# Two joined transformer blocks on one core: experts that add into the residual, and a layer norm inside the next feed-forward

## The reference, cut to what matters

```python
x = layer_norm(ALPHA * x + (1 + gt1) * mix, ln1_g, ln1_b)     # ALPHA = 2 ** 0.25
h = x * (1 + sc2) + sh2
ffn = moe_ffn(h, router_w, router_b, w1, b1, w2, b2)          # 32 experts, 1024 -> 2048 -> 1024
x = layer_norm(ALPHA * x + (1 + gt2) * ffn, ln2_g, ln2_b)
# second model, two layers
h = rmsnorm(x, ffn1_norm[i])
x = x + 0.5 * (silu(h @ wg) * (h @ wu)) @ wd                  # 1024 -> 2816 -> 1024
x = x + mixing(rmsnorm(x, mix_norm[i]), positions, ...)       # fox, dilated (rope), hgrn2
x = x + 0.5 * swiglu(rmsnorm(x, ffn2_norm[i]))
# layer_norm: (x - mean) / sqrt(var + 1e-5) * g + b ; rmsnorm: x / sqrt(mean(x*x) + 1e-6) * g
# softmax over layers of hgrn_lower_bounds, and cos/sin of positions: computed once ("tables")
```

## Time and profile before

| | |
|---|---|
| median of 3 runs | 2408.95 us (2402.76 to 2416.14) |
| profiled execution | span 2405.4 us, first to last instruction; no time of its own is shown beside it |
| TensorE (PE) busy | 2217.6 us, 92% |
| VectorE (DVE) busy | 1085.6 us, 45% |
| ScalarE (ACT) busy | 709.9 us, 30% |
| DMA | 626.63 MB, mean 261 GB/s; about 425 GB/s in the expert stage |

### The profile page before, as it was taken

The page is one execution under the profiler, slowest core; times in us unless marked ns, Lnnn a source line. Parts: engine busy times, 40 slices in busy tenths (PEclk is TensorE's granted clock), DMA queues, the critical chain, the costliest instruction groups (busy, mean ns, idle before and its releaser), DMA issues. The chain is left out here.

```text
span 2405.4 us, 37789 instructions
## 1 busy us (share of the span) xinstructions
PE 2217.6 (92%) x15750; PEld 1605.7 (67%) x15750; DVE 1085.6 (45%) x1633; ACT 709.9 (30%) x899; POOL 18.7 (1%) x17
## 2 busy tenths in 40 slices
PE   6987879999999999999996999999999999999998
PEld 4746743443333333333335999988999999988997
DVE  4548342121111111111115656677656656677664
ACT  3343231111111111111114444445334434445332
POOL 0002000000000000000000000000000000000000
PEclk8968989999999999999998999999999999999999
DMA  9630269999999999999985455424555555424551
GB/s 391 241 158 27 69 281 424 424 425 426 425 425 425 425 425 425 425 426 425 418 334 169 158 192 175 134 95 140 193 182 168 193 187 181 139 90 140 194 188 56
DMA packets 233056, 626.63 MB, mean 261 GB/s; under 512 B 13144, under 2 KB 149880, under 8 KB 197112
## 3 DMA queue, kind: packets, MB, share of 16 engines
q1 hardware_dynamic: 229736, 622.06, 67.2%
q10 hardware_dynamic: 3216, 3.06, 0.4%
HBM read 624.03 MB, written 1.05 MB: 260 GB/s over the span
## 5 line engine op out<-in xcount | busy, mean ns | idle before, releaser
L1916 DVE TENSOR_TENSOR w_low<-ring,w_high 128x2048 fp32r<-128x2048 f32 x168 | 383.8, 2290 | 274.9 <-ACT w_high L1911 274.9
L1911 ACT ACTIVATE w_high<-ring 128x2048 fp32r<-128x2048 f32 x168 | 319.8, 1909 | 269.7 <-PE bank L2125 136.6
L1672 PE MATMUL bank<-ring,ut 128*64 128x512 f32 x1024 | 250.6, 642 | 47.2 <-DMA ring<-in_exp_w_dram 47.2
L1643 PE MATMUL bank<-ring_odd,xt 128*64 128x512 f32 x1024 | 225.0, 597 | 0.0
L1643 PE MATMUL bank<-ring,xt 128*64 128x512 f32 x1024 | 223.3, 594 | 0.3 <-ACT xt L1726 0.3
L1672 PEld LDWEIGHTS bank<-ring,ut 128*64 128x64 f32 x1024 | 73.5, 146 | 208.6 <-issue 126.7
L2140 PE MATMUL bank<-h_high,w_high 128*128 128x256 f32 x1408 | 186.8, 281 | 16.0 <-ACT h_high L2013 16.0
L2140 PEld LDWEIGHTS bank<-h_high,w_high 128*128 128x128 f32 x1408 | 175.4, 189 | 16.8 <-ACT h_high L2013 16.6
L2140 PE MATMUL bank<-h_high,w_low 128*128 128x256 f32 x1408 | 185.9, 280 | 0.0
L2140 PE MATMUL bank<-h_low,w_high 128*128 128x256 f32 x1408 | 185.8, 280 | 0.0
L1730 ACT ACTIVATE sg<-glu 128x512 f32<-128x512 f32 x32 | 20.2, 630 | 537.4 <-DVE glu L1793 537.4
(11 more groups left out here) (532 smaller groups left out, 2871.3 us busy)
## 6 DMA issues: line engine op xcount, KB each, us to landing
ring<-in_exp_w_dram SPq DMA_DIRECT2D x256, 1024.0 KB, 21.8
ring_odd<-in_exp_w_dram SPq DMA_DIRECT2D x128, 1024.0 KB, 20.7
ring<-in_ffn_w_gate_dram SPq DMA_DIRECT2D x44, 1024.0 KB, 5.2
ring<-in_ffn_w_up_dram SPq DMA_DIRECT2D x44, 1024.0 KB, 5.2
ring<-in_ffn_w_down_dram SPq DMA_DIRECT2D x44, 1024.0 KB, 4.8
ring<-in_w_in_dram SPq DMA_DIRECT2D x36, 1024.0 KB, 5.3
ring<-in_ada_w_dram SPq DMA_DIRECT2D x24, 1024.0 KB, 12.3
ring<-in_w_out_dram SPq DMA_DIRECT2D x8, 1024.0 KB, 5.2
```

What stands on the lines that cost most here:

```text
L1643: ins = nc.tensor.matmul(bank[b][at:at + SLOTS, :], xt[:, c, SLOTS * side:SLOTS * side + SLOTS], (ring, ring_odd)[side][:, c, 512 * q:512 ...
L1672: ins = nc.tensor.matmul(bank[2 + dh][64 * dh:64 * dh + 64, :], ut[:, r % 4, 64 * (r // 4):64 * (r // 4) + 64], w[:, x, 512 * dh:512 * dh ...
L1911: nc.scalar.activation(w_bufs[0][u % BUFS], ring2[:, u % RING2, :], ACT.Copy).then_inc(high2, 1)
L1916: nc.vector.tensor_tensor(w_bufs[1][u % BUFS], ring2[:, u % RING2, :], w_bufs[0][u % BUFS].bitcast(F32), ALU.subtract).then_inc(low2, 1)
```

## The change

1. *Experts add into the scaled residual.* ALPHA is folded into the first norm's gain and bias (`x_gain`), the cleared accumulator is gone (its memset too), and each piece of `back` is now added by two operations of 128x256, piece times `mod` plus `xT`.
2. *Last second weights in first-weight slots.* The second weights of experts 30 and 31 go to `ring` slots 0 to 7 and wait for expert 30's first weights to be used, instead of slots 8 to 11 behind the second weights before them.
3. *Second layer norm inside the first feed-forward.* Stage c9 is gone. `opening` runs in the feed-forward's stage: VectorE halves the sum over chunks twice, so the mean is 2 products instead of 8; pairs of squares are added, so the variance is 4 instead of 8. Gain and bias of the norm times the RMS gain (`open_gain`) give `h_high` straight from the scaled `xT`; gain and bias are applied to `xT` by VectorE for even chunks and by ScalarE for odd ones.
4. *Tables over four units.* The tables are cut into four parts behind units 29 to 32; ScalarE's two functions come behind unit 32. `rope_tables` is cut in two for it.

```diff
@@ -1491,12 +1489,13 @@
+                act.wait_ge(sem("x_gain_ready"), 1)
-                    nc.scalar.activation(xT[:, c, :], xT[:, c, :], ACT.Identity, bias=par("ln1_b", c), scale=par("ln1_g", c))
+                    nc.scalar.activation(xT[:, c, :], xT[:, c, :], ACT.Identity, bias=x_gain[:, 1, c:c + 1], scale=x_gain[:, 0, c:c + 1])
...
@@ -1504,6 +1503,8 @@
+                nc.vector.tensor_scalar(x_gain[:, 0, :], par("ln1_g", 0, DC), ALPHA, None, ALU.mult)
+                st.tell(nc.vector.tensor_scalar(x_gain[:, 1, :], par("ln1_b", 0, DC), ALPHA, None, ALU.mult), "x_gain_ready")
@@ -1599,17 +1600,27 @@
-                    load_down(E - 2)
-                    load_down(E - 1)
+                    for k in range(8):
+                        sp.wait_ge(used, p * (8 * E) + (8 * E + (U_EXP - 16 + k + 1)))
+                        src = A["exp_w2"][0, E - 2 + k // 4, T * (k % 4):T * (k % 4) + T, :]
+                        sp.dma_start(slot3(k, 2), src.rearrange("(x p) n -> p x n", p=P)).then_inc(loaded[k], 16)
-                        load_up(E, 0)
+                        for k in range(8):
+                            sp.wait_ge(used_down, p * (4 * E) + (4 * (E - 2) + k + 1))
+                            sp.dma_start(ring[:, k, :], A["exp_w1"][0, 0, P * k:P * k + P, :]).then_inc(loaded[k], 16)
-                    def landed(k, e):
-                        pe.wait_ge(loaded[k], p * (16 * E) + (e * 16 + 16 * (loads_into(k, U_EXP) + 1)))
+                    def down_slot(e, k):
+                        if isinstance(e, int) and e >= E - 2:
+                            slot = 4 * (e - (E - 2)) + k
+                            pe.wait_ge(loaded[slot], p * (8 * E + 16) + (8 * E + 16 * (loads_into(slot, U_EXP) + 1)))
+                            return slot
+                        pe.wait_ge(loaded[8 + k], p * (16 * (E - 2)) + (e * 16 + 16 * (loads_into(8 + k, U_EXP) + 1)))
+                        return 8 + k
@@ -1664,8 +1675,7 @@
-                            landed(8 + k, e)
-                            w = slot3(8 + k, 2)
+                            w = slot3(down_slot(e, k), 2)
@@ -1804,8 +1814,11 @@
-                            av = flat(acc[:, 2 * n:2 * n + 2, :])
-                            nc.vector.tensor_tensor(av, bank[6 + n % 2][:, :], av, ALU.add).then_inc(sem("acc_added"), 1)
+                            for j in range(2):
+                                m = 2 * n + j
+                                ins = nc.vector.scalar_tensor_tensor(xT[:, m, :], bank[6 + n % 2][:, T * j:T * j + T], mod[:, 40 + m:41 + m], xT[:, m, :],
+                                                                     ALU.mult, ALU.add)
+                            ins.then_inc(sem("acc_added"), 1)
@@ -1914,52 +1927,6 @@
-        with ExitStack() as c9, Stage(nc, pool) as S:
...
-            ln_pe, ln_act, ln_dve = layer_norm(S, xT, root[:, :], sq, (0, 1))
...
-                ln_pe(pe)
...
-                    nc.scalar.activation(xT[:, 4 * j:4 * j + 4, :], xT[:, 4 * j:4 * j + 4, :], ACT.Copy, scale=ALPHA).then_inc(sem("x_scaled"), 1)
-                split_high(act, 0)
-                ln_act(act)
...
-                split_high(act, 1)
...
-                    st.tell(nc.vector.scalar_tensor_tensor(xT[:, m, :], acc[:, m, :], mod[:, 40 + m:41 + m], xT[:, m, :],
...
-                split_low(dve, 0)
-                ln_dve(dve, st)
-                split_low(dve, 1)
...
@@ -2073,7 +2041,77 @@
-        def ffn(S, f, L, base_unit, norm_name, first, flip, update, after, tables=None):
+        def opening(S, f):
+            sem = S.sem
+            mean, var = bank[6][:, 0:T], bank[7][:, 0:T]
+            halves = qp[:, :, :]
+            def tensor(pe):
+                pe.wait_ge(sem("halves_added"), 2)
+                for c in range(2):
+                    ins = nc.tensor.matmul(mean, ones, halves[:, c, :], start=(c == 0), stop=(c == 1))
+                ins.then_inc(sem("mean_ready"), 1)
+                for c in range(4):
+                    pe.wait_ge(sem("pairs_added"), c // 2 + 1)
+                    ins = nc.tensor.matmul(var, ones, squares[:, 4 * (c // 2) + c % 2, :], start=(c == 0), stop=(c == 3))
+                ins.then_inc(sem("var_ready"), 1)
+            def scalar(act):
+                for j in range(4):
+                    act.wait_ge(sem("centered"), j + 1)
+                    nc.scalar.activation(squares[:, 2 * j:2 * j + 2, :], xT[:, 2 * j:2 * j + 2, :], ACT.Square).then_inc(sem("squares"), 1)
+                split_high(act, 0)
+                act.wait_ge(sem("var_ready"), 1)
+                nc.scalar.activation(root[:, :], var, ACT.Sqrt, bias=1e-5, scale=1.0 / D).then_inc(sem("root_ready"), 1)
+                for c in range(DC):
+                    act.wait_ge(sem("scaled"), c // 2 + 1)
+                    nc.scalar.activation(h_parts[0][:, c, :], xT[:, c, :], ACT.Identity, bias=open_gain[:, 1, c:c + 1],
+                                         scale=open_gain[:, 0, c:c + 1]).then_inc(sem(f + "h_high"), 1)
+                    if c % 2:
+                        nc.scalar.activation(xT[:, c, :], xT[:, c, :], ACT.Identity, bias=par("ln2_b", c), scale=par("ln2_g", c)
+                                             ).then_inc(sem("x_odd"), 1)
+                split_high(act, 1)
+                for j in range(4):
+                    act.wait_ge(sem("x_even"), j + 1)
+                    act.wait_ge(sem("x_odd"), j + 1)
+                    nc.scalar.activation(squares[:, 2 * j:2 * j + 2, :], xT[:, 2 * j:2 * j + 2, :], ACT.Square).then_inc(sem(f + "squares"), 1)
+            def vector(dve):
+                st = Steps(dve, sem, "dve_step")
+                st.tell(nc.vector.memset(fox_bias[:, :], 0.0), "bias_cleared")
+                st.step(nc.vector.tensor_tensor(halves, xT[:, 0:4, :], xT[:, 4:8, :], ALU.add), "halves_added")
+                st.step(nc.vector.tensor_tensor(halves[:, 0:2, :], halves[:, 0:2, :], halves[:, 2:4, :], ALU.add), "halves_added")
+                for k, name in enumerate(("ln2_g", "ln2_b")):
+                    nc.vector.tensor_tensor(open_gain[:, k, :], par(name, 0, DC), par("ffn1_norm_2", 0, DC), ALU.mult)
+                dve.wait_ge(sem("mean_ready"), 1)
+                for j in range(4):
+                    xj = xT[:, 2 * j:2 * j + 2, :]
+                    st.tell(nc.vector.scalar_tensor_tensor(xj, mean.unsqueeze(1).to_broadcast([P, 2, T]), -1.0 / D, xj, ALU.mult, ALU.add), "centered")
+                for k in range(2):
+                    dve.wait_ge(sem("squares"), 2 * k + 2)
+                    st.tell(nc.vector.tensor_tensor(squares[:, 4 * k:4 * k + 2, :], squares[:, 4 * k:4 * k + 2, :], squares[:, 4 * k + 2:4 * k + 4, :],
+                                                    ALU.add), "pairs_added")
+                dve.wait_ge(sem("root_ready"), 1)
+                st.step(nc.vector.reciprocal(root[:, :], root[:, :]))
+                for j in range(4):
+                    xj = xT[:, 2 * j:2 * j + 2, :]
+                    st.tell(nc.vector.tensor_tensor(xj, xj, root[:, :].unsqueeze(1).to_broadcast([P, 2, T]), ALU.mult), "scaled")
+                    if j == 1:
+                        split_low(dve, 0)
+                for c in range(DC):
+                    dve.wait_ge(sem(f + "h_high"), c + 1)
+                    if c % 2:
+                        dve.wait_ge(sem("x_odd"), c // 2 + 1)
+                    else:
+                        st.step(nc.vector.tensor_scalar(xT[:, c, :], xT[:, c, :], par("ln2_g", c), par("ln2_b", c), ALU.mult, ALU.add), "x_even")
+                    nc.vector.scalar_tensor_tensor(h_parts[1][:, c, :], xT[:, c, :], par("ffn1_norm_2", c), h_parts[0][:, c, :].bitcast(F32),
+                                                   ALU.mult, ALU.subtract).then_inc(sem(f + "h_low"), 1)
+                split_low(dve, 1)
+            return tensor, scalar, vector
+        def ffn(S, f, L, base_unit, norm_name, first, flip, update, after, tables=None, opens=None):
@@ -2177,16 +2217,19 @@
-                parts_high(act)
+                if opens:
+                    opens[1](act)
+                else:
+                    parts_high(act)
-                if tables:
-                    tables[0](act)
+                    if tables and n == FFN_UNITS - 1:
+                        tables[0](act)
@@ -2228,18 +2271,21 @@
-                parts_low(dve, update)
+                if opens:
+                    opens[2](dve)
+                else:
+                    parts_low(dve, update)
-                if tables:
-                    tables[1](dve)
+                    if tables:
+                        tables[1](dve, n - (LOOP_AT + REPS * LOOP2))
@@ -2764,30 +2810,35 @@
-            def vector(dve):
-                st = Steps(dve, sem, "table_step")
-                dve.wait_ge(small, 16 * 9)
+            def vector(dve, part):
+                st = Steps(dve, sem, f"table_step{part}")
```

(27 more changed lines are left out.)

75 lines of the change are left out of this document (28 added, 47 removed).

## The result

Twenty runs of each kernel: before 2405.58 us (2401.23 to 2418.53), after 2392.44 us (2385.30 to 2401.69), ratio 0.9940, 95% interval 0.9926 to 0.9954. The median is 13.1 us lower, and the interval of the ratio stands for 11 to 18 us; 13.8 had been forecast from the profile, and 2395 as the time.

A forecast was written before the change was run, and what follows sets the result against it. Weights' DMAs pace the expert stage, TensorE what follows, where other work shows as holes. Opening with tail 10.3 plus tables 3.5 gave 13.8 us off, span 2391.6, time 2395; own range 2392 to 2399, with rivals A, B, D and scatter 2384 to 2407.

The forecast's parts named there:

- Expert tail: End of the expert stage: longer adds against new slots' -0.8 us; 0.45 us later at worst, range -0.4 to +1.3.
- The adds' term: Adds behind the expert loop: +0.5 us at the last but one back, +0.45 at the last add.
- Adds in the loop: Expert loop: some 0.5 us a back reaches TensorE but goes into the DMA wait of 3.0 us for two experts.
- Rival C: Expert loop: adds uncovered, 1.25 us in each of 16 pairs, 20 us less 13.8, time 2415; chance 0.05.
- Opening: Second layer norm to first feed-forward's unit 2: 10.3 us won, tail included, between 7 and 12.
- that is the last wait, and unit 1 starts there: First feed-forward: VectorE's low part of unit 1, ready at 1296.8, is what unit 1 waits for.
- the 0.5 us wait for the squares: First feed-forward, end of unit 1: squares' adds ready at 1303.0, unit 1 ends at 1302.5, a new wait.
- Rival A: Opening wins only 5.6 us through slower handovers and half clock into unit 1; total 9, time 2400; chance 0.15.
- The table load: Opening, ScalarE: the skill's 1.38 us drain would delay the root 1.0 us, win 9.3; the trace spoke against it.
- Tables: Feed-forward: 7.05 us gone before the loop, 3.5 back at the mixing's start (1.4 to 4.2), net 3.5.
- rival B: End of feed-forward: tables only move their hole, all 7.2 us shows, net 0, total 10, time 2399; chance 0.09.
- Rival D: Clock kept and part 2 hidden at mixing start, opening at upper end: 17.6 us, 2391 or down to 2387; chance 0.10.

The follow-up runs named there:

- experiment 4: Kernel after with the last second weights back in slots 8 to 11; expert tail 44.54 us against 43.00, last down unit 8.62 against 7.09.
- kernel 3: Kernel after with each pair of adds into `xT` preceded by a useless pair into `hT`; expert stage 937.2 us against 932.3.
- kernels 5: Kernel after with unit 0's low part on VectorE before the reciprocal, while it waits for the root; opening 30.76 us, 1.95 less.
- 7: Kernel after with useless products keeping TensorE busy in the opening; opening 31.09 us, 1.6 less than the profile of after.
- 10: Kernel after with early low part, moved table parts and useless TensorE products together; median 2389.61 us, ratio to before 0.9937, opening 31.14.
- the five profiles: Profiles of the kernel after, its unchanged repeat, and the kernels with doubled adds, old slots and two moved table parts; opening 31.6 to 32.7 us.
- Kernel 6: Kernel after with tables' part 2 ahead of the loop and part 3 behind the mixing's update; unit 2 through mixing's first unit 4.2 us less.
- the repeat: Kernel after, unchanged, run again; median 2392.30 us, ratio to before 0.9941, opening 31.67 us.
- the full sums: Kernel after with mean and variance again as 8 products each, without VectorE's halves and pair adds; opening 32.45 us.
- the tables alone: Kernel before with only the tables in four parts taken from the kernel after; span 2396.0 us, opening 42.38 us.

## Why the prediction was right, point by point

- **Expert tail**, +0.45 us forecast "at worst", though its own terms, 0.5 + 0.45 - 0.8, sum to 0.15: -0.4 in the traces, at the lower end of the range given. The slots' term was right: the last down unit took 7.09 us (7.1) and lost 0.82 (0.8). The adds' term was too large: 0.43 us and not 0.95 (experiment 4).
- **Adds in the loop**, nothing: right (kernel 3). Rival C fell.
- **Opening**, 10.3 us with the tail: 9.7 and 0.4, together 10.1. By steps, in us behind VectorE's start, forecast and measured: centring 3.9 and 4.13; root 10.7 and 11.08; first `h_low` 17.8 and 18.35; low part of unit 1 ready 25.1 and 25.15; unit 1's start 25.1 and 26.81; unit 2's start 31.7 and 32.71. The failed step is "that is the last wait, and unit 1 starts there": I had charged unit 0 with 1.5 us for half clock, by the unit of before, which was back at full rate 3.6 us behind its first matmul. Here that took 10.1 us. From the first matmul with `h_low` TensorE needed 7.92 us for 44 of unit 0's 48 matmuls, which at full rate are 5.2 (an estimate, 44/48 of 5.65), so half clock cost some 2.7 us. TensorE was last by 1.7 us, and for that reason the 0.5 us wait for the squares did not appear (kernels 5, 7, 10). The size is partly chance: in the five profiles with this opening TensorE was last by 0.6 to 1.7 us. Rival A, 5.6 us, fell: its handovers did not grow.
- That 10.3 and 10.1 agree so well is in part luck. The walk had the memset 0.45 us later and the opening 10.7 us shorter; it was only 9.7 shorter, and the tail, 0.8 us better than forecast, made up for most of that.
- By place, the 9.7 us are three parts: the reciprocal starts 11.50 us behind the memset instead of 16.69; unit 0's first matmul starts 3.17 us behind the reciprocal instead of 12.45; and from there to unit 2 it takes 18.04 us instead of 13.24. The last part is a loss.
- Unit 2 begins 34.2 us behind the end of the last add, 44 before. "32" had been announced, but the walk itself gives 33.3, since 1.6 us lie between the last add and VectorE's start.
- **The table load.** The estimate by the Trainium skill ("ScalarE: Activation LUTs", what ACT_TABLE_LOAD costs) had the root 1.0 us later. The trace says no: the load at 1271.45 ends at 1272.73, the root waits for TensorE until 1273.44. At the other load of this stage no drain shows either:

```profile
1467.56 1.28 ACT L2811 ACT_TABLE_LOAD   x1
...
1468.85 0.21 ACT L2811 ACTIVATE soft<-soft 128x8 f32<-128x8 f32 x1
```

- **Tables**, 7.05 gone, 3.5 back, net 3.5: net 3.0. The hole before the loop and its half rate went, the u parts came 0.3 us ahead of unit 32 (1464.53 against 1464.86), so rival B fell. Back came 2.7 of wait (2.76 forecast) and 1.5 of clock, the upper bound of 4.2 and not 3.5: the clock cost its full price. Kernel 6 gets all of it back. Rival D, which had the clock kept there and VectorE never last in the opening, did not come.
- **The time**: 13.8 forecast from the sum, 13.1 measured; in the trace 12.9 behind the memset and 11.8 from the experts on (11.3 and 11.8 in the repeat's profile). 2392.44 lies 2.6 below the forecast because the median of before was 2405.58 in twenty runs and 2408.95 in the three that I had.

Not tried: the cut barrier alone, apart from the new order in it. So how the 9.7 us divide between the two stays open; only the share of the shortened sums is bounded, at most some 0.8 us.

## What to carry to other kernels

Where TensorE works in short bursts, price its next dense stretch with several us at half clock (3.6 us from its first matmul in the kernel before, 7.8 to 10.1 in the five profiles with the new opening), and ask of every cut in TensorE's work whether it saves time or only lowers the clock. Work that is moved off one hole lands in another unless the place has slack before a consumer: put it behind the operation that the waiting engine needs (the table's last part behind the update), not ahead of it. And compare traces by stretches between common points before crediting a span to a change, and learn from repeats how far each stretch scatters by itself.

## What the runs showed of the hardware that was not expected

The first 340 us are nearly the same program in all kernels, but in the profile of before they took 340.1 us and after 330.0. Some 7.3 us of this sit in an attention stretch where TensorE is not quite dense. Window of before, then of after:

```profile
145.00:150.00 5.00, 4.42 (x14) 2.91 (x14) 2.28 (x8) 1.48 (x5) 0.00 (x0) 0.50 0.59 251
```

```profile
145.00:150.00 5.00, 3.84 (x22) 2.62 (x21) 3.70 (x13) 2.56 (x10) 0.00 (x0) 1.00 0.02 8
```

The stretch from 138 us took 31.2 us in the kernel before, at a mean clock of 0.53; its like from 135 us in the kernel after took 23.9 at 0.86. All twelve profiles fall into these two groups, with nothing between: 31.2 to 31.5 us in three (before, the old slots, the full sums) and 23.8 to 23.9 in nine. The time to the experts goes with them. It is 330 to 335 us in the same nine profiles, that of the tables alone among them, whose first stages are those of before (333.9); 342.8 with the old slots and 346.5 with the full sums, though neither edit touches that stretch. TensorE at half clock is busy for longer with the same work, and it can stay there for some 30 us, or not, from one execution to the next. This is the likeliest source of the scatter of about 15 us among runs of one kernel. The runs without a profile bear it out in part, since each has its mean granted clock: of the twenty runs of the kernel after, the ten fastest (up to 2391.9 us) have 0.962 to 0.966 and the ten slowest 0.956 to 0.961, and the correlation of time and clock is -0.95. They do not tell in which stretch the clock was lost.
